# Stick-breaking suffix sums as one-pass products of split values, with the masks added to the scores by TensorE

## What is computed

```python
z = q @ k.T * scale                                   # 256 queries, 256 keys, head width 64
mask = kpos[None, :] < qpos[:, None]
log_1m = where(mask, -softplus(z), 0.0)
suffix = cumsum(log_1m, axis=keys, reverse=True) - log_1m
att = where(mask, exp(log_sigmoid(z) + suffix), 0.0)
out = att @ v
```

## Time and profile before

| | us |
|---|---|
| median of three runs | 1674.56 |
| profiled execution, its own time | 1675.27 |
| its span, first to last instruction | 1673.4 |
| TensorE busy | 1625.0 (97%) |
| VectorE busy | 1397.6 (84%) |
| ScalarE busy | 1122.2 (67%) |
| GpSimd busy | 108.1 (6%) |
| mean granted TensorE clock | 0.991 of 2.4 GHz |

### The profile page before, as it was taken

How to read it: one execution, slowest core, us unless ns; L and a number is a source line. 1 busy time by engine, 2 the same in 40 slices (tenths; PEclk the granted TensorE clock), 3 DMA queues, 4 the chain that set the end, 5 groups by cost and what they waited for, 6 DMA issues and landing times.

```text
span 1673.4 us, 23549 instructions
## 1 busy us (share of the span) xinstructions
PE 1625.0 (97%) x7850; PEld 1339.6 (80%) x7850; DVE 1397.6 (84%) x1691; ACT 1122.2 (67%) x1389; POOL 108.1 (6%) x209
## 2 busy tenths in 40 slices
PE   8999989999989998899999999999999999999996
PEld 6977768888879776788888888888888888888885
DVE  7977777787687567798988989989989989989987
ACT  4665454344455564578878878778778778778784
POOL 0120010000011101620000000000000000000000
PEclk9999999999999999899999999999999999999999
DMA  9955547777568344599999999999999999999993
GB/s 386 390 233 217 186 154 298 279 267 283 201 238 361 132 150 150 204 373 361 355 377 364 365 374 361 359 376 359 366 367 363 374 363 363 368 369 378 350 368 121
DMA packets 74014, 514.85 MB, mean 308 GB/s; under 512 B 9108, under 2 KB 10333, under 8 KB 12254
## 3 DMA queue, kind: packets, MB, share of 16 engines
q1 hardware_dynamic: 72226, 508.64, 79.8%
q0 software_dynamic: 1152, 4.19, 0.7%
q10 hardware_dynamic: 572, 1.18, 0.2%
HBM read 511.88 MB, written 2.11 MB: 307 GB/s over the span
## 4 chain that ended last, share of the span: by engine, by line
PE 88%; DVE 4%; ACT 3%; issue 3%; POOL 1%; DMA 0%; DVEq 0%; ACTq 0%; POOLq 0%
PE ps L1426 27%; PE ps L1428 26%; PE ps L1427 26%; PE ps L1708 2%; DVE wlo L318 1%; ACT whi L310 1%; DVE raw L327 1%; ACT vals L711 1%; PE ps L1570 1%; DVE qk L1027 1%; PE ps L1590 0%; PE ps L1448 0%; PE ps L1903 0%; PE ps L1876 0%; PE ps L1904 0%
## 5 line engine op out<-in xcount | busy, mean ns | idle before, releaser
L318 DVE TENSOR_TENSOR wlo<-raw,whi 128x1024 fp32r<-128x1024 f32 x868 | 1015.9, 1221 | 148.0 <-ACT whi L310 147.7
L310 ACT ACTIVATE whi<-raw 128x1024 fp32r<-128x1024 f32 x868 | 867.6, 1053 | 211.1 <-PE ps L1428 208.5
L1426 PE MATMUL ps<-whi,hhi 128*128 128x512 f32 x1568 | 624.5, 398 | 11.1 <-DVE hlo L839 5.0
L1428 PE MATMUL ps<-wlo,hhi 128*128 128x512 f32 x1568 | 612.8, 391 | 0.0
L1427 PE MATMUL ps<-whi,hlo 128*128 128x512 f32 x1568 | 612.6, 391 | 0.0
L1426 PEld LDWEIGHTS ps<-whi,hhi 128*128 128x128 f32 x1568 | 295.2, 188 | 78.0 <-issue 8.7
L1428 PEld LDWEIGHTS ps<-wlo,hhi 128*128 128x128 f32 x1568 | 295.0, 188 | 63.1
L1427 PEld LDWEIGHTS ps<-whi,hlo 128*128 128x128 f32 x1568 | 295.5, 188 | 59.2 <-issue 1.1
L1426 PE MATMUL ps<-whi,ohi 128*128 128x512 f32 x432 | 173.5, 402 | 2.3 <-issue 2.3
L1428 PE MATMUL ps<-wlo,ohi 128*128 128x512 f32 x432 | 169.2, 392 | 0.0
L1427 PE MATMUL ps<-whi,olo 128*128 128x512 f32 x432 | 168.6, 390 | 0.0
(11 more groups left out here) (222 smaller groups left out, 1091.8 us busy)
## 6 DMA issues: line engine op xcount, KB each, us to landing
raw<-in_w_moe SPq DMA_DIRECT2D x336, 1024.0 KB, 6.9
raw<-in_w_pre_moe SPq DMA_DIRECT2D x98, 1024.0 KB, 4.9
raw<-in_w_mod_units SPq DMA_DIRECT2D x48, 1024.0 KB, 5.3
x<-in_x SPq DMA_DIRECT2D x2, 512.0 KB, 4.8
bias<-dist_scratch SPq DMA_DIRECT2D x1, 1024.0 KB, 9.7
xn_rows<-wide ACTq DMA_DIRECT2D x2, 512.0 KB, 4.5
out<-x SPq DMA_DIRECT2D x1, 512.0 KB, 2.6
out<-x SPq DMA_DIRECT2D x2, 256.0 KB, 2.1
```

The lines of the kernel that those rows point to most:

```text
L310: nc.scalar.activation(whi[:, s % SPLIT, part], raw[:, slot(s), part], ACT.Copy).then_inc(hi_done, 1)
L318: nc.vector.tensor_tensor(wlo[:, s % SPLIT, part], raw[:, slot(s), part], whi[:, s % SPLIT, part].bitcast(F32), ALU.subtract).then_inc(lo_ ...
L1426: nc.tensor.matmul(out, a_hi, b_hi, start=first, stop=False, **kw)
L1428: return nc.tensor.matmul(out, a_hi, b_lo, start=False, stop=last, **kw)
```

## The change

The selects on GpSimd in the mixers go. A constant `later` (0 where the key comes before the query, -1e30 elsewhere) is added to both diagonal blocks of the scores by TensorE, as a product of the identity with `later` in fp32r, 128 columns each. With z at -1e30 the later steps give a softplus of zero and a weight of zero by themselves.

VectorE now computes softplus twice, in fp32 into `at2` and rounded to fp32r into `lm_hi`, waits for its own four results, and subtracts to get `lm_lo`. The suffix sums are taken with four fp32r products per head instead of two fp32 ones. `lm_hi` and `lm_lo` lie in parts of `ohi` and `olo` that are free then. Four constants are copied to fp32r once, by VectorE, ahead of `first_norm`; GpSimd makes one constant more at the start.

```diff
@@ after_arg, ScalarE
-                            nc.scalar.activation(at2[:, p % 2, s, :], z, ACT.Exp).then_inc(sb_att, 1)
+                            nc.scalar.activation(at2[:, p % 2, s, :], z, ACT.Exp).then_inc(at_done, 1)
@@ after_scores, VectorE
                             dve.wait_ge(sb_ln, 4 * l + p + 1)
-
+                            links[0] += 2
                             nc.vector.scalar_tensor_tensor(at_p[:, s, :], z[:, 0:384], 0.0, eb[:, s, :], ALU.max,
-                                                           ALU.add).then_inc(sb_sum, 1)
+                                                           ALU.add).then_inc(dve_link, 1)
+                            nc.vector.scalar_tensor_tensor(lm_hi[:, s, :], z[:, 0:384], 0.0, eb[:, s, :],
+                                                           ALU.max, ALU.add).then_inc(dve_link, 1)
...
+                    if p < 4:
+                        dve.wait_ge(dve_link, links[0])
                     for s in range(2):
-                        if p >= 4:
+                        if p < 4:
+                            nc.vector.tensor_tensor(lm_lo[:, s, :], at_p[:, s, :], lm_hi[:, s, :].bitcast(F32),
+                                                    ALU.subtract).then_inc(sb_lm, 1)
+                        else:
@@ start, VectorE
             for c in range(C):
                 normed(0, c)
+            for whole, part in ((ident[:], identR), (lower, lowerR), (nones, nonesR), (later, laterR)):
+                nc.vector.tensor_copy(part[:], whole).then_inc(onepass, 1)
@@ mixer, GpSimd
-            def keep_earlier(p, s, fill_done):
-
-                select(at2[:, p % 2, s, 0:P], ALU.is_gt, 1, -1, 0, 0.0)
-                select(at2[:, p % 2, s, S:384], ALU.is_gt, 1, -1, 0, 0.0).then_inc(fill_done, 1)
...
-            mixer(0)
...
-            mixer(1)
@@ scores, TensorE
                             nc.tensor.matmul(z[:, 0:S], kT[:, 0:P], qT, start=True, stop=True)
                             nc.tensor.matmul(z[:, S:384], kT[:, P:S], qT[:, P:S], start=False, stop=True,
+                                             skip_group_check=True)
+
+                            nc.tensor.matmul(z[:, 0:P], identR[:], laterR[:], start=False, stop=True,
+                                             skip_group_check=True)
+                            nc.tensor.matmul(z[:, S:384], identR[:], laterR[:], start=False, stop=True,
                                              skip_group_check=True).then_inc(z_done, 1)
@@ arguments, TensorE
-                            nc.tensor.matmul(z[:, 0:384], lower[:], at2[:, p % 2, s, :], start=False, stop=True,
-                                             skip_group_check=True)
-                            nc.tensor.matmul(z[:, P:S], nones[:], at2[:, p % 2, s, S:384], start=False, stop=True,
-                                             skip_group_check=True).then_inc(arg_done, 1)
+                            for part in (lm_hi[:, s, :], lm_lo[:, s, :]):
+                                nc.tensor.matmul(z[:, 0:384], lowerR[:], part, start=False, stop=True,
+                                                 skip_group_check=True)
+                                ins = nc.tensor.matmul(z[:, P:S], nonesR[:], part[:, S:384], start=False, stop=True,
+                                                       skip_group_check=True)
+                            ins.then_inc(arg_done, 1)
```

More of the change, by code:

```diff
@@ L126, in build @@
         silu = qk[:, C * NB:2 * C * NB].rearrange("p (c n) -> p c n", c=C)
+        lm_hi = ohi[:, 4:7, :].rearrange("p k t -> p (k t)").rearrange("p (s n) -> p s n", s=2)
+        lm_lo = olo[:, 4:7, :].rearrange("p k t -> p (k t)").rearrange("p (s n) -> p s n", s=2)
         yhi = ohi[:, :, P:2 * P]
@@ L133, in build @@
         eb = sb("eb", [P, 2, 384])
+        lower = eb[:, 0, 0:P]
+        later = eb[:, 0, P:2 * P]
+        nones = eb[:, 0, 2 * P:3 * P]
         at2 = sb("at2", [P, 2, 2, 384])
@@ L137, in build @@
         upper = sb("upper", [P, P])
-        lower = sb("lower", [P, P])
         ones = sb("ones", [P, P])
         iota = sb("iota", [P, P])
+        identR = sb("identR", [P, P], F32R)
+        lowerR = sb("lowerR", [P, P], F32R)
+        nonesR = sb("nonesR", [P, P], F32R)
+        laterR = sb("laterR", [P, P], F32R)
         modT = sb("modT", [P, DEPTH * MODS])
-        nones = sb("nones", [P, P])
         colsB = sb("colsB", [P, 64])
@@ L204, in build @@
         const = sem("const")
+        onepass = sem("onepass")
         relx_set = sem("relx_set")
@@ L226, in build @@
         sb_ln = sem("sb_ln")
-        sb_sum = sem("sb_sum")
         sb_lm = sem("sb_lm")
         arg_done = sem("arg_done")
-        sb_att = sem("sb_att")
         mo_max = sem("mo_max")
@@ L1054, in _ @@
             nc.vector.memset(ones[:], 1.0).then_inc(const, 1)
-            nc.vector.memset(nones[:], -1.0).then_inc(const, 1)
+            nc.vector.memset(nones, -1.0).then_inc(const, 1)
             nc.vector.memset(posI[:], -1.0).then_inc(const, 1)
             nc.vector.memset(wI[:], 0.0).then_inc(const, 1)
-            dve.wait_ge(const, 9)
+            dve.wait_ge(const, 10)
             link(nc.vector.tensor_scalar(rank[:], ids[:], 1.0 / 16, None, ALU.mult))
@@ L1283, in _ @@
                            allow_small_or_imprecise_dtypes=True).then_inc(const, 1)
-            for tile in (ident, upper, lower):
-                nc.gpsimd.memset(tile[:], {"ident": 0.0, "upper": 1.0, "lower": -1.0}[tile.name]).then_inc(pool_link, 1)
+            for tile, value in ((ident[:], 0.0), (upper[:], 1.0), (lower, -1.0), (later, 0.0)):
+                nc.gpsimd.memset(tile, value).then_inc(pool_link, 1)
                 links[0] += 1
@@ L1296, in _ @@
             select(upper[:], ALU.is_gt, 1, -1, 0, 0.0).then_inc(const, 1)
-            select(lower[:], ALU.is_ge, -1, 1, 0, 0.0).then_inc(const, 1)
+            select(lower, ALU.is_ge, -1, 1, 0, 0.0).then_inc(const, 1)
+            select(later, ALU.is_gt, 1, -1, 0, NEG).then_inc(const, 1)
             def inv_rms(done, src, at_col, *add):
@@ L1547, in scores @@
                 def scores(p):
+                    if p == 0:
+                        pe.wait_ge(onepass, 4)
                     for s in range(2):
@@ L1795, in _ @@
             base_of = {2: FFN_BASE[0], 1: FFN_BASE[1]}
-            pe.wait_ge(const, 9)
+            pe.wait_ge(const, 10)
             pe.wait_ge(small_in, 16 * 2)
```

## The result

The changed kernel takes 1681.17 us (median of 7 runs, 1679.44 to 1682.95) against 1674.56 before: a ratio of 1.0041, 95% interval 1.0030 to 1.0052. It is 6.6 us slower. The forecast was a loss of 5.0 (1679.6, range 1674 to 1686.5): the sign fits, and the loss is a third larger. The profiled execution took 1682.87 us with a span of 1681.1, 7.7 more than before's.

A forecast was written before the change was run, and what follows sets the result against it. TensorE was taken to bound the kernel, with GpSimd hidden. A pair's +0.54 us gave +4.3 over 8 pairs; with 0.5 of VectorE stalls and 0.2 at the start, +5.0, or 1679.6 us, range 1674 to 1686.5.

The forecast's parts named there:

- What bounds the kernel: Whole kernel: TensorE sets the pace, busy 1625 of 1673 us; GpSimd's selects are hidden, so dropping them wins nothing.
- Suffix products: TensorE, each pair: fp32 sums of 1.74 us become fp32r products, 0.175 us per 384 columns and n per 128.
- The price n: TensorE: an fp32r product of 128 columns costs 0.12 us, range 0.065 to 0.22.
- Rival (a): Narrow fp32r products on TensorE cost what fp32 costs, 0.22 us each: 1686.0 us in all; chance 0.17.
- What the masks do to the scores: TensorE, each pair: masks between the heads end the scores' overlap, +0.42 us, and add changes of +0.20; together 0 to 0.62.
- masks of 0.48: TensorE, each pair: four more products of 128 columns for the masks, 4n = 0.48 us.
- changes of 0.20: TensorE, each pair: going from whole-array work to half-array scores and back is paid once more, +0.20 us, 0 to 0.20.
- VectorE: Softplus and subtractions add 2.0 us a pair, +1.8 net; stalls for `olo` 0.5 us in the first mixer, none in the second.
- Rival (d): VectorE becomes the bound in the first mixer, waits for `olo` grow, +3.5 us on the forecast: 1683.1; chance 0.10.
- Start: VectorE at the start: four constant copies of 0.2 us each, 0.6 of 0.8 hidden by waits: +0.2 us, 0 to 0.9.
- Sum: Whole kernel: 4.3 on TensorE, 0.5 of stalls and 0.2 at the start make +5.0 us, 1679.6.

The follow-up runs named there:

- e9: Kernel before without GpSimd's 64 selects in the mixers, nothing in their place, so the causal mask is left out: 1674.82 us, ratio to before 1.0003.
- e1: Changed kernel with the four mask products of a pair moved behind the scores of both heads: 1673.91 us, ratio to before 0.9994.
- e4: Changed kernel with each head's two mask products issued twice, 32 narrow fp32r products more: 1685.19 us, ratio to before 1.0063.
- e5: As e1, with the two masks of a head made into one product of 256 columns: 1672.29 us, ratio to before 0.9984.
- e10: Changed kernel with its mask products in fp32 instead of fp32r, at the same place between the heads: 1684.58 us, ratio to before 1.0066.
- e8: Kernel before plus VectorE's additional work alone, two softplus passes and two subtractions a pair into tiles nobody reads: 1675.85 us, ratio to before 1.0004.
- e6: As e5, with VectorE's `olo` split at the even places moved ahead of the conditioning columns of its unit: 1669.57 us, ratio to before 0.9967.
- e7: Kernel before with only the move of `olo` ahead of the conditioning columns: 1672.25 us, ratio to before 0.9983.
- e3: Changed kernel with masks kept but suffix sums in two fp32 products per head from one softplus on VectorE: 1684.8 us, ratio to before 1.0068.
- e2: Changed kernel without its mask products, so the causal mask of the stick-breaking heads is left out: 1670.86 us, ratio to before 0.9974.

## Why the prediction was right, and where it was off

**What bounds the kernel**: right. The time followed TensorE's own work in the step in the experiments that changed it, and GpSimd's release was worth nothing (e9). The dense part stayed as long as before, as it was to: 310.7 and 310.8 us from the last MoBA scores of the first mixer to its last addition. Behind the router it is 0.6 longer in the profile (see the sum below).

**Suffix products**: right in the sum, a little too dear, and not in the two terms. A 384 and a 128 together take 0.29 (79.76 to 80.05) for a forecast 0.295, the first two of them 0.23. But the starts split it as 0.23 behind the product of 384 columns and 0.06 behind the one of 128, not as 0.175 and 0.12. That the two misses cancel is luck; why the starts lie so, no run shows. The gain was 0.65 a pair against 0.56.

**The price n**: right for the masks. 0.12 was chosen between 0.065 and 0.22 by the router's row; e1 and e4 show 0.11 to 0.12 in a stream (0.16 for the first behind the scores), and e5 that it is the load of the weights. Rival (a), which had a chance of 0.17, is out. The Trainium skill's 81 ns for 128 columns ("TensorE: Matmul & The Clock Gate", "Back-to-back issue gap") would, as an estimate, have given e4 2.6 us. The starts of 0.11 to 0.12 speak against it here; the measured 4.0 fits them better but can't decide alone. Its rule that a load overlaps a running product only where the row group differs (same page, "What overlaps and what doesn't") is contradicted once more by products of 128 columns 0.11 apart: load (0.11 by the router's row) and columns (0.05 at 2.4 GHz) one after the other would need 0.16, by estimate.

**What the masks do to the scores**: the step that was mis-sized. The mechanism, an overlap lost because the masks stand between the heads, was forecast. e1 shows that the place costs it and e10 that the kind, fp32 or fp32r, doesn't. Its size was put at 0.42, "serially 1.28 ... but the pair takes 0.86". The 1.28 was worked out at the pace of whole-array fp32 products, 0.64 a head. The head alone takes 0.85, so two take 1.70 and the loss is 0.85. The pair before had no partial overlap but a complete one. The missing 0.21 a head can be read from the starts: a head alone spends 0.54 on its 256 columns (80.71 to 81.25) and 0.31 on its 128 (81.25 to 81.56), where that pace gives 0.43 and 0.21; record by record it is 0.32, 0.22, 0.11 and 0.20. So each stretch of half-array products costs 0.11 more where it begins and 0.10 more where it ends. The pair before paid this once for both heads, inside its 0.86; the prediction took the 0.86 for work alone, and so read 0.42 of overlap where there was 0.64, and beside the changes that it did count (0.20) it missed the 0.21 that a second stretch pays inside. The other terms of this part were close: masks of 0.48 and changes of 0.20 were forecast, and 0.58 is left of the 1.43 when the 0.85 is taken off. Per pair it is +0.78 against +0.54, over eight pairs 1.9 us; the wait for `olo` and the start came out 0.3 cheaper than forecast, so the loss is 1.6 us larger than forecast.

**VectorE**: right. +2.0 us a pair, the wait ahead of pair 5 forecast at 0.3 beyond the spare is 0.38, in all 0.4 against 0.5, none in the second mixer. Rival (d) is out by e8 and by the changed kernel's own waits, which in the mixers grew by these 0.38 alone.

**Start**: forecast +0.2; the profiles show 0 to 0.17. A copy takes 0.14 from start to start, not 0.2, and what hides them is an idle time of 0.46 that the prediction didn't see, not the two of 0.30 and 0.28 that it named, which are as long as before.

**Sum**: 6.2 + 0.4 = 6.6 by the trace, and 6.6 between the medians. That they agree to the tenth is partly luck, for the profiled executions differ by 7.7. From stretch to stretch they show: the first mixer's scores start 0.5 earlier; the first mixer is 3.6 longer and the second 3.1, which are the forecast places, together 6.7; 0.9 arises between the last addition of the dense part (line 867, now 873) and the first scores of the second mixer, and 0.6 behind the router's products. The windows of the changed kernel show a mean granted clock of 0.70 and 0.87 in the stretch of the 0.9, so a part of it ran at 1.2 GHz; TensorE had been busy 2.05 of the 4 us before:

```profile
468.00:472.00 4.00, 2.05 (x8) 1.05 (x6) 3.46 (x5) 3.42 (x6) 1.74 (x3) 1.00 0.00 0
472.00:476.00 4.00, 3.32 (x10) 2.58 (x11) 3.54 (x4) 0.68 (x2) 2.48 (x2) 0.70 0.56 195
476.00:480.00 4.00, 3.55 (x18) 2.64 (x16) 1.50 (x6) 2.19 (x6) 0.00 (x0) 0.87 0.79 330
```

The profiled execution of before has 1.00 in all windows of that stretch, with TensorE busy for 2.42 to 3.47 of each 4 us. From that addition to those scores it is 53.8 us in six of the twelve profiles (the changed kernel, e1, e4, e6, e7, e9), all with such a fall of the clock, and 53.0 in the other six, all without.

A second stretch like it lies inside the first mixer, behind the 2.02 us for which TensorE waits ahead of the scores of pair 6. In before's profile the weight products there ran at 1.2 GHz, in e3's, behind the same wait, at 2.4:

```profile
141.20:144.40 3.20, 3.20 (x9) 2.43 (x9) 2.70 (x12) 2.65 (x9) 0.00 (x0) 0.50 0.59 251
```

```profile
146.40:149.60 3.20, 3.20 (x16) 2.63 (x15) 2.70 (x12) 2.66 (x9) 0.00 (x0) 1.00 0.58 246
```

From the scores of pair 6 to those of pair 7 it is 12.9 us with the fall (before, the changed kernel, e2, e8, e9) and 11.3 without (e1, e3, e4, e5, e10). e6 and e7, which have no such wait, have 11.3 too. So these two falls move a single execution by 0.9 and 1.6 us, and spans of single profiles can't be compared without looking for them. Falls that come and go like these are of the size by which the medians of e2, e3 and e8 miss their forecasts (1.1, 0.8 to 1.2, and 1.0); which of them a median holds can't be said, since only one execution of each kernel is profiled. Why the clock falls in one execution and not in the next, no run shows.

## What to carry to other kernels

Work that is put on a saturated engine costs by where it stands, not only by how long it is: four short products, two of them between the half-array products of two heads, cost 7.3 us more over eight places than the same four behind both heads. Before adding an instruction between two others, look at what these two take together and what one of them takes alone; an overlap that nobody wrote down shows only in that comparison. And price a narrow product by its weight load: two narrow ones on the same weights, made into one wide one, were about half as dear here (over the kernel without masks, 0.38 us a pair in e1 and 0.18 in e5).

## What the runs showed of the hardware that was not expected

The fp32 scores of two heads, with a contraction over partitions 0 to 63 and 64 to 127, one behind the other, cost together what one head's cost alone: 0.86 us for two heads, 0.85 for one. In each such stretch the first record takes 0.11 more and the last 0.10 more than the pace of whole-array products gives. In a stream, an fp32r product of 128 columns takes 0.11 to 0.12 us from start to start, about the same as one of 256; behind half-array products it takes 0.16 and 0.22. One wait of 2.02 us was followed by a stretch at 1.2 GHz that cost a further 1.6 us in five profiles, and by none in five others.
